# Prompt attention by pairs of heads, with the weights normalised by a diagonal in their transposes

## The chip, the core and the metric

The kernel runs on one core of a Trainium2 chip. The metric is the time of one execution on the device in microseconds. The core has TensorE (PE; its weight loads are PEld), VectorE (DVE), ScalarE (ACT), GpSimd (POOL) and SyncE (SP, which issues DMAs). They run side by side, each through its own instructions in order, and wait for each other on semaphores.

## The reference

One layer of a decoder for a prompt of 1024 tokens and 8 sampled sequences of 8 tokens, all f32, d_model 1024: an S5 state-space group and an attention with forget gates side by side, one output projection over both, then a mixture of 64 experts. What the change touches is the attention over the prompt (8 heads of 64) and the norm of its output:

```python
s = jnp.einsum('bqhd,bkhd->bhqk', q, k).astype(jnp.float32) * (HEAD_DIM ** -0.5)
s = s + jnp.transpose(cq, (0, 2, 1))[..., :, None] - jnp.transpose(ck, (0, 2, 1))[..., None, :]
causal = k_pos[None, :] <= q_pos[:, None]
s = jnp.where(causal, s, -jnp.inf)
p = jax.nn.softmax(s, axis=-1)
o = jnp.einsum('bhqk,bkhd->bqhd', p.astype(v.dtype), v)
...
merged = jnp.concatenate([_rmsnorm(y_ssm, g_ssm_out), _rmsnorm(o, g_attn_out)], axis=-1)
out = merged.astype(h.dtype) @ w_out
```

`cq` and `ck` are the running sums of the log forget values at queries and keys.

## The kernel before

The whole step is one program, its order on every engine written out by hand. The stages follow each other: state-space group, projections to q, k and v, attention over the prompt, attention of the sampled sequences over their pages, output projection, second norm, router, shared expert, routed experts.

PSUM is cut into six slots: 0 and 1 of two banks (1024 columns), 2 to 5 of one (512). `fill` makes TensorE wait until a slot's last content has been drained, `full` and `empty` count fillings and drainings, `wait_full` and `wait_empty` wait for a named one.

The attention over the prompt goes through 64 iterations `ATT`, for each head the eight query tiles i = 0 to 7, of (i + 1) x 128 keys. Four engines share one:
- TensorE (L714 to L748): `logits(it + 2)` into slot 0 or 1, with the whole 128 rows of `qT` (each head's copy of q has zeros in the other head's 64 rows) against `kT` of two heads; then, after a wait for the exponential, the transposes of the weights (L743, slots 2 and 3, four blocks each); then `weigh(it - 1)` (L728): transposed weights as stationary operand, v of 64 columns as moving one, into slot 4 or 5.
- VectorE (L1299 to L1320): logits plus running sum of the query minus that of the keys (L1313), the causal mask on the last 128 columns (L1316), the maximum (L1317), and the reciprocal of the previous iteration's sum (L1303).
- ScalarE (L1785 to L1812): the exponential with its sum (L1792, from `sc` into `pr`), the copies of the transposed weights (L1809), and the copy of the output of the iteration before, scaled by 1/sum (L1799), into `o_tok` (tokens by channels).
- `neg_c`, the keys' negated sums of one head spread over 128 partitions, is made once per head at i = 3: TensorE spreads it by an 8-row product into a logits slot (L707), ScalarE copies it (L1783).

GpSimd does nothing in this stage; before it, it clears `qT`, after it `q_bd` (L2016, the block-diagonal q of the samples), and later scales `w_out` by the norm's gains (L2021). The sampled sequences run through eight iterations (L784 to L813). Behind them, TensorE does the first half projection of tile 0 (`project_out(0, 0)`, the state-space half), while ScalarE squares `o_tok` (L1846), VectorE scales it by 1/rms (L1383), TensorE transposes it (L839) and ScalarE copies it into `oT` (L1853). Then come the other half projections (L830), two of 16 records per token tile. SyncE issues the shared expert's loads (L2184 to L2186) once the transposes are done. TensorE's first use of them is L864, in the third round of the second norm.

## Time and profile before

| | before |
|---|---|
| three runs | 2373.78, 2384.41 (median), 2386.98 us |
| the profiled execution | 2372.85 us, span 2371.1 us |
| PE busy | 2078.4 us (88%) |
| DVE, ACT, POOL busy | 892.5, 533.7, 300.3 us |

### The profile page before, as it was taken

Reading aid. Unit: us, or ns where it says so; the run is one execution under the profiler, and the core shown is the slowest. Engines: PE = TensorE matmul, PEld = TensorE weight load, DVE = VectorE, ACT = ScalarE, POOL = GpSimd, SP = SyncE. Lnnn points to the kernel's source line nnn. Section 1 sums busy time; section 2 is a strip of 40 time slices with the busy share of each in tenths; the row PEclk is TensorE's granted clock in tenths of the full one; section 3 lists DMA queues with packets and bytes.
Section 4 is the critical chain, followed back from the end, with each engine's and each line's share of the span. In section 5 each row is a group of like instructions: output and inputs, shape, how many; then the busy total and the mean of one; then the engine's idle time right before and its main releaser. Section 6 shows DMA issues by size and latency. Waiting matters only on the chain.

```text
span 2371.1 us, 28991 instructions
## 1 busy us (share of the span) xinstructions
PE 2078.4 (88%) x8262; PEld 1117.0 (47%) x8263; DVE 892.5 (38%) x2450; ACT 533.7 (23%) x993; POOL 300.3 (13%) x236
## 2 busy tenths in 40 slices
PE   4797899998888888978978999899899999998990
PEld 1456555446666334545434444444445455544450
DVE  2827400315554222234423333333333333333338
ACT  3423221015544112033111111111111111111122
POOL 0010100000000030000001122122122222221124
PEclk7898889999998998988988999999899999999995
DMA  9531200022000443001148899899888778898843
GB/s 335 218 155 23 113 0 1 0 76 58 18 1 18 131 138 133 0 19 58 52 176 279 288 298 293 277 295 297 265 273 250 250 241 259 266 288 281 287 102 137
DMA packets 100878, 394.20 MB, mean 166 GB/s; under 512 B 27279, under 2 KB 30003, under 8 KB 71996
## 3 DMA queue, kind: packets, MB, share of 16 engines
q1 hardware_dynamic: 70020, 302.44, 34.4%
q0 software_dynamic: 24768, 90.19, 15.9%
q10 hardware_dynamic: 6024, 0.73, 0.2%
q8 instruction: 38, 0.62, 0.1%
q14 instruction: 28, 0.23, 0.0%
HBM read 329.16 MB, written 62.57 MB: 165 GB/s over the span
## 4 chain that ended last, share of the span: by engine, by line
PE 27%; DMA 22%; issue 5%; SPq 4%; DVE 2%; ACT 1%; POOL 0%; POOLq 0%; DVEq 0%; ACTq 0%
DMA arena<-in_w_exp_down 22%; PE psum L961 11%; PE psum L989 5%; PE psum L830 5%; SPq L2209 2%; PE psum L947 1%; SPq L2204 1%; SPq L2205 1%; DVE arena L1607 1%; PE psum L858 1%; PE psum L864 1%; DVE arena L1617 1%; PE psum L871 0%; PE psum L809 0%; PE psum L854 0%
## 5 line engine op out<-in xcount | busy, mean ns | idle before, releaser
L961 PE MATMUL psum<-arena 128*128 x1360 | 631.1, 619 | 55.2 <-SPq L2230 51.5
L961 PEld LDWEIGHTS psum<-arena 128*128 128x128 f32 x1360 | 261.1, 197 | 358.3 <-issue 358.3
L989 PE MATMUL psum<-arena,tail 128*128 x672 | 302.3, 592 | 0.0
L2057 POOL DMA_INDIRECT moe_rows<-arena x84 | 133.4, 1588 | 815.2 <-ACT arena L1941 291.4
L1563 DVE TENSOR_TENSOR arena<-arena,psum 128x256 f32<-128x256 f32 x85 | 35.8, 421 | 499.2 <-ACT arena L1927 499.2
L989 PEld LDWEIGHTS psum<-arena,tail 128*128 128x128 f32 x672 | 121.1, 190 | 120.5 <-issue 120.5
L1927 ACT ACTIVATE arena<-psum 128x256 f32<-128x256 f32 x85 | 32.7, 385 | 644.3 <-PE psum L961 644.3
L678 PE MATMUL psum<-arena 128*128 128x512 f32 (+1 forms) x384 | 126.5, 493 | 0.0
L830 PE MATMUL psum<-arena 128*128 128x512 f32 (+1 forms) x288 | 124.3, 593 | 0.9 <-ACT arena L1853 0.5
L1541 DVE TENSOR_TENSOR arena<-tail,arena 128x1152 bf16<-128x1152 f32 x89 | 119.6, 1344 | 0.0
L1941 ACT ACTIVATE arena<-psum,arena 128x512 f32<-128x512 f32 x84 | 57.7, 687 | 213.3 <-PE psum L989 213.3
L947 PEld LDWEIGHTS psum<-tail,arena 128*128 128x128 f32 x688 | 81.1, 142 | 52.2 <-issue 44.8
L1590 DVE TENSOR_SCALAR arena<-psum,arena 128x512 f32<-128x512 f32 x84 | 63.1, 751 | 95.9 <-PE psum L989 95.9
L1922 ACT ACTIVATE arena<-psum 128x1024 f32<-128x1024 f32 x86 | 88.1, 1024 | 48.9 <-PE psum L947 48.9
L719 PE MATMUL psum<-arena 128*128 128x512 f32 (+2 forms) x192 | 86.9, 569 | 10.4 <-ACT arena L1783 10.4
L947 PE MATMUL psum<-tail,arena 128*128 128x128 f32 x688 | 90.1, 274 | 6.5 <-DMA arena<-h_rows,arena 6.5
L830 PEld LDWEIGHTS psum<-arena 128*128 128x128 f32 (+1 forms) x288 | 68.5, 239 | 55.3 <-issue 40.1
L2044 POOL DMA_INDIRECT arena<-h_rows,arena x88 | 86.6, 984 | 59.4 <-issue 32.2
L678 PEld LDWEIGHTS psum<-arena 128*128 128x128 f32 x384 | 63.8, 193 | 62.6 <-issue 62.6
L728 PE MATMUL psum<-arena 128*128 128x64 f32 x576 | 77.2, 284 | 0.0
L728 PEld LDWEIGHTS psum<-arena 128*128 128x128 f32 x576 | 75.3, 206 | 0.0
L544 PE MATMUL psum<-arena 128*128 128x512 f32 (+1 forms) x144 | 65.0, 604 | 0.0
(486 smaller groups left out, 2342.1 us busy)
## 6 DMA issues: line engine op xcount, KB each, us to landing
arena<-in_w_exp_gate SPq DMA_DIRECT2D x64, 1024.0 KB, 5.3
arena<-in_w_exp_up SPq DMA_DIRECT2D x64, 1024.0 KB, 9.4
arena<-in_w_exp_down SPq DMA_DIRECT2D x64, 1024.0 KB, 12.3
arena<-in_w_ada SPq DMA_DIRECT2D x24, 1024.0 KB, 7.6
arena<-in_w_ada_final SPq DMA_DIRECT2D x8, 1024.0 KB, 6.5
arena<-in_cache_k SPq DMA_DIRECT2D x32, 256.0 KB, 3.4
arena<-in_cache_v SPq DMA_DIRECT2D x32, 256.0 KB, 2.9
arena<-in_w_in SPq DMA_DIRECT2D x1, 6176.0 KB, 18.5
```

The source lines that it names most:

```text
L544: ins = pe.matmul(slot[2 + t % 2][0:rows(t), :], tile_of(hT, t, k), w_u[:, k, :], start=(k == 0), stop=(k == KD - 1))
L678: ins = pe.matmul(slot[b][:, 0:c1 - c0], w_q[:, k, w * DA + j * P:w * DA + (j + 1) * P], hT[:, k, c0:c1], start=(k == 0), stop=(k == KD - 1))
L719: ins = pe.matmul(slot[it % 2][:, c0:c1], qT[:, h, i * P:(i + 1) * P], kT[:, h // 2, c0:c1], start=True, stop=True)
L728: ins = pe.matmul(slot[4 + it % 2][:, 0:DH], pt[:, it % 2, j * P:(j + 1) * P], v[:, j, h * DH:(h + 1) * DH], start=(j == 0), stop=(j == i))
L830: ins = pe.matmul(slot[half][0:rows(t), n * 512:(n + 1) * 512], lhs, w_out[:, half * KA + k, n * 512:(n + 1) * 512], start=(k == 0), stop= ...
L947: ins = pe.transpose(slot[0][:, k * P:(k + 1) * P], x_rows[:, par, k * P:(k + 1) * P], ident)
L961: ins = pe.matmul(slot[2 + par].rearrange("p (h n) -> p h n", h=2), xTs[:, par, k, :], ring_gu[:, at, :, k, :].rearrange("p a h n -> p (a ...
L989: ins = pe.matmul(slot[1][:, n * 512:(n + 1) * 512], hTs[:, k, :], ring_d[:, at, k, n, :].rearrange("p a n -> p (a n)"), start=(k == 0), s ...
L1541: tt(onehot[:, par], iota_row.unsqueeze(1).to_broadcast([P, NT, P]), blk_rank[:, par].unsqueeze(2).to_broadcast([P, NT, P]), ALU.is_equal) ...
L1922: f(xTs[:, par].rearrange("p k c -> p (k c)"), slot[0], ACT.Copy).then_inc(xt_copied, 1)
L2044: pool.indirect_dma_start(x_rows[:, par, :], None, h2_dram, bass.IndirectOffsetOnAxis(ap=g_idx[:, par:par + 1], axis=0)).then_inc(gathered ...
L2057: pool.indirect_dma_start(y_dram, bass.IndirectOffsetOnAxis(ap=s_idx[:, par:par + 1], axis=0), y_buf[:, par, :], None, compute_op=ALU.add) ...
```

## The change

The attention goes by pairs of heads j (two heads share the 128 rows of `qT` and `kT`) and, within a pair of heads, by tiles of falling width, i = 7 to 0: 32 pairs p, 64 numbers it = 2 p + a.
- Logits: one product of 64 rows for each head, in alternation, head a in slot a. `qT` has no zeros any more (the clearing by GpSimd and half of ScalarE's q copies go).
- The mask: GpSimd adds it to the 128 diagonal columns of `neg_c` before each tile (falling widths make this sound), of which there are now four buffers; VectorE's add of it goes.
- The exponential works in place in `sc` (four buffers). VectorE makes the reciprocal of the sum behind its add for the next pair, GpSimd multiplies the identity by it (`over_sum`), and TensorE's products of the weights with this diagonal transpose and normalise them.
- Weighing: v is the stationary operand (64 columns) and the transposed weights the moving one; the two heads write the two halves of the 128 PSUM partitions, so the output is in `oT` (channels by tokens) with one copy per pair.
- The spreading of the sums is cut in halves of 512 columns, in slots 4 and 5: four ahead of the loop, the others behind the pairs with i = 6, 5, 4, 3.
- The norm: `o_tok`, its squares, its scaling and its transposes go, but for the 64 sampled rows (`o_smp`). GpSimd squares `oT` and adds over the channels' four blocks under the sampled sequences, TensorE sums over partitions with eight products of one column in iteration b = 4, and VectorE multiplies the attention half of the projection by 1/rms where it adds it.
- SyncE issues the shared expert's loads behind the last projection instead of ahead of the second.

The core of the diff; runs of removed lines are left out, the functions above show them.

```diff
-        qT = arena(21536, H, T)
+        qT = arena(21536, KA, T)
         v = arena(30240, NT, DA)
         kT = arena(41248, KA, T)
         k_tok = arena(45600, 2, DA)
         lf = arena(46624, T, parts=H)
         lf_a = arena(47712, T, parts=H)
...
+        sc = arena(8192, 4, SEQ)
+        pt = arena(25888, 4, SEQ)
+        oT = arena(14336, KA, T)
+        o_smp = arena(18944, DA, parts=NS)
+        o_acc = arena(39200, SEQ)
+        o_pow = arena(40512, 512)
+        over_sum = arena(40512, 4, P)
         c_row = arena(18944, T, parts=H)
-        neg_c = [arena(20032, SEQ), arena(39200, SEQ)]
+        neg_c = [arena(20032, SEQ), arena(39200, SEQ), arena(12288, SEQ), arena(13312, SEQ)]
...
-        ATT = [(i, h) for h in range(H) for i in range(8)]
+        PAIRS = [(i, j) for j in range(KA) for i in range(7, -1, -1)]
...
+        SPREAD_AT = (6, 5, 4, 3)
+        def pt_keys(p):
+            return range(0, PAIRS[p][0] + 1, 4)
+        def spread_of(p):
+            i, j = PAIRS[p]
+            if j + 1 == KA or i not in SPREAD_AT:
+                return None
+            a, n = divmod(SPREAD_AT.index(i), 2)
+            return 2 * (j + 1) + a, n
...
+            def spread_sums(h, n, s_):
+                fill(pe, ("CB", h, n), s_)
+                full(pe.matmul(slot[s_], ident[0:H, h:h + 1].to_broadcast([H, P]), c_row[:, n * 512:(n + 1) * 512], start=True, stop=True), ("CB", h, n))
+            for i in range(4):
+                spread_sums(i // 2, i % 2, 4 + i % 2)
             slots.wait_empty(pe, ("V", 7))
...
+            def logits(p):
+                i, j = PAIRS[p]
+                for a in range(2):
+                    fill(pe, ("L", 2 * p + a), a)
                 for c0 in range(0, (i + 1) * P, 512):
                     c1 = min(c0 + 512, (i + 1) * P)
...
+                    for a in range(2):
+                        h0, h1 = a * DH, (a + 1) * DH
+                        ins = pe.matmul(slot[a][:, c0:c1], qT[h0:h1, j, i * P:(i + 1) * P], kT[h0:h1, j, c0:c1], start=True, stop=True)
+                        if c1 == (i + 1) * P:
+                            full(ins, ("L", 2 * p + a))
+            def turn_weights(p, a):
+                i, j = PAIRS[p]
+                it = 2 * p + a
+                pe.wait_ge(pn_ready, it + 1)
+                for q0 in pt_keys(p):
                     b = 2 + (q0 // 4)
                     fill(pe, ("PT", it, q0), b)
-                    for j in range(q0, min(q0 + 4, i + 1)):
-                        ins = pe.transpose(slot[b][:, (j - q0) * P:(j - q0 + 1) * P], pr[:, it % 2, j * P:(j + 1) * P], ident)
+                    for m in range(q0, min(q0 + 4, i + 1)):
+                        ins = pe.matmul(slot[b][:, (m - q0) * P:(m - q0 + 1) * P], sc[:, it % 4, m * P:(m + 1) * P], over_sum[:, it % 4, :], start=True, stop=True)
                     full(ins, ("PT", it, q0))
...
+            def weigh(p):
+                i, j = PAIRS[p]
+                fill(pe, ("O", p), 4 + p % 2)
+                for m in range(i + 1):
+                    for a in range(2):
+                        if m % 4 == 0:
+                            slots.wait_empty(pe, ("PT", 2 * p + a, m))
+                        ins = pe.matmul(slot[4 + p % 2][a * DH:(a + 1) * DH, 0:P], v[:, m, (2 * j + a) * DH:(2 * j + a + 1) * DH],
+                                        pt[:, (2 * p + a) % 4, m * P:(m + 1) * P], start=(m == 0), stop=(m == i), skip_group_check=True)
+                full(ins, ("O", p))
+            logits(0)
+            for p in range(len(PAIRS)):
+                if p + 1 < len(PAIRS):
+                    logits(p + 1)
+                turn_weights(p, 0)
+                if p:
+                    weigh(p - 1)
+                turn_weights(p, 1)
+                if spread_of(p):
+                    spread_sums(*spread_of(p), 4 + (p + 1) % 2)
+            weigh(len(PAIRS) - 1)
...
+                if b == 4:
+                    pe.wait_ge(o_squares, 1)
+                    fill(pe, "OSS", 4)
+                    for t in range(8):
+                        ins = pe.matmul(slot[4][:, t:t + 1], o_acc.rearrange("p (c t) -> p t c", t=CH)[:, t], ones_col, start=True, stop=True)
+                    full(ins, "OSS")
...
+            slots.wait_empty(pe, "SR")
+            fill(pe, "OT", 2)
+            for k in range(KA):
+                ins = pe.transpose(slot[2][:, k * P:k * P + NS], o_smp[:, k * P:(k + 1) * P], ident[0:NS, 0:NS])
+            full(ins, "OT")
             for t in range(NT):
                 if t:
                     project_out(t, 0)
+                if t == 8:
+                    slots.wait_empty(pe, "OT")
...
             def one_over_sum(it):
                 dve.wait_ge(p_ready, it + 1)
                 if it >= 4:
...
+                    dve.wait_ge(pn_ready, it - 3)
+                dve.reciprocal(att_one[:, 8 + it % 4:9 + it % 4], att_one[:, 4 + it % 4:5 + it % 4]).then_inc(recip_ready, 1)
+            for p, (i, j) in enumerate(PAIRS):
                 n = (i + 1) * P
...
+                for a in range(2):
+                    it = 2 * p + a
+                    full(dve, ("L", it))
+                    dve.wait_ge(c_masked, it + 1)
+                    if it >= 4:
+                        full(dve, ("PT", it - 4, pt_keys(p - 2)[-1]))
+                    empty(stt(sc[:, it % 4, 0:n], slot[a][:, 0:n], c_tok[:, i * H + 2 * j + a:i * H + 2 * j + a + 1], neg_c[(2 * j + a) % 4][:, 0:n], ALU.add, ALU.add), ("L", it))
+                    if p:
+                        one_over_sum(it - 2)
+                for a in range(2):
+                    it = 2 * p + a
+                    slots.wait_empty(dve, ("L", it))
+                    dve.tensor_reduce(att_one[:, it % 4:it % 4 + 1], sc[:, it % 4, 0:n], AX.X, ALU.max, negate=True).then_inc(s_ready, 1)
+            for it in (2 * len(PAIRS) - 2, 2 * len(PAIRS) - 1):
+                one_over_sum(it)
...
+            dve.wait_ge(o_sq, 1)
             dlink(ts(ssq, ssq, 1.0 / DA, EPS, ALU.mult, ALU.add))
             dve.sem_inc(x_var, 1)
             dve.wait_ge(x_std, NXG + 1)
             dlink(dve.reciprocal(rstd, rstd))
...
-                ins = tt(mix, mix, slot[1][0:m, :], ALU.add)
+                ins = stt(mix, slot[1][0:m, :], rstd[0:m, t:t + 1], mix, ALU.mult, ALU.add)
...
+            def spread_out(h, n):
+                full(act, ("CB", h, n))
+                if h >= 4:
+                    act.wait_ge(s_ready, 16 * (h // 2 - 1))
+                empty(f(neg_c[h % 4][:, n * 512:(n + 1) * 512], slot[slots.use[("CB", h, n)][0]], ACT.Copy, scale=-1.0), ("CB", h, n))
             def exponentials(it):
-                n = (ATT[it][0] + 1) * P
+                n = (PAIRS[it // 2][0] + 1) * P
                 act.wait_ge(s_ready, it + 1)
-                if it >= 2:
-                    full(act, ("PT", it - 2, pt_keys(it - 2)[-1]))
                 if it >= 4:
                     act.wait_ge(recip_ready, it - 3)
...
+                f(sc[:, it % 4, 0:n], sc[:, it % 4, 0:n], ACT.Exp, bias=att_one[:, it % 4:it % 4 + 1],
+                  accum_out=att_one[:, 4 + it % 4:5 + it % 4]).then_inc(p_ready, 1)
+            def weights_out(it):
+                p = it // 2
+                for q0 in pt_keys(p):
+                    w = min(4, PAIRS[p][0] + 1 - q0) * P
                     full(act, ("PT", it, q0))
...
+                    if p >= 2:
+                        full(act, ("O", p - 2))
+                    empty(f(pt[:, it % 4, q0 * P:q0 * P + w], slot[2 + q0 // 4][:, 0:w], ACT.Copy), ("PT", it, q0))
+            def attention_out(p):
+                i, j = PAIRS[p]
+                full(act, ("O", p))
+                empty(f(oT[:, j, i * P:(i + 1) * P], slot[4 + p % 2][:, 0:P], ACT.Copy), ("O", p))
+            for i in range(4):
+                spread_out(i // 2, i % 2)
+            for p in range(len(PAIRS) + 1):
+                for a in range(2):
+                    if p < len(PAIRS):
+                        exponentials(2 * p + a)
+                    if p:
+                        weights_out(2 * p - 2 + a)
+                if p >= 2:
+                    attention_out(p - 2)
+                if p and spread_of(p - 1):
+                    spread_out(*spread_of(p - 1))
+            attention_out(len(PAIRS) - 1)
...
+            slots.wait_empty(act, "SR")
+            slots.wait_empty(act, "OSS")
+            f(sq_o[0:NS, :], o_smp, ACT.Square, accum_out=ssq[0:NS, 8:9]).then_inc(o_sq, 1)
...
+            def mask(p):
+                i, j = PAIRS[p]
+                for a in range(2):
+                    h = 2 * j + a
+                    if i == 7:
+                        slots.wait_empty(pool, ("CB", h, 0))
+                        slots.wait_empty(pool, ("CB", h, 1))
+                    else:
+                        slots.wait_empty(pool, ("L", 2 * p - 2 + a))
+                    diag = neg_c[h % 4][:, i * P:(i + 1) * P]
+                    pool.tensor_tensor(diag, diag, causal, ALU.add).then_inc(c_masked, 1)
+            def spread_diagonal(it):
+                pool.wait_ge(recip_ready, it + 1)
+                if it >= 4:
+                    slots.wait_full(pool, ("PT", it - 4, pt_keys(it // 2 - 2)[-1]))
+                pool.tensor_scalar(over_sum[:, it % 4, :], ident, att_one[:, 8 + it % 4:9 + it % 4], None, ALU.mult).then_inc(pn_ready, 1)
+            for p in range(len(PAIRS) + 1):
+                if p < len(PAIRS):
+                    mask(p)
+                if p:
+                    spread_diagonal(2 * p - 2)
+                    spread_diagonal(2 * p - 1)
+            slots.wait_full(pool, ("O", len(PAIRS) - 1))
             plink(pool.memset(q_bd[:, :, :, :], 0.0))
             pool.sem_inc(smp_pool, 1)
+            slots.wait_empty(pool, ("O", len(PAIRS) - 1))
+            slots.wait_empty(pool, ("O", len(PAIRS) - 2))
+            for n in range(2):
+                cols = slice(512 * n, 512 * (n + 1))
+                plink(pool.tensor_tensor(o_acc[:, cols], oT[:, 0, cols], oT[:, 0, cols], ALU.mult))
+                for j in range(1, KA):
+                    plink(pool.tensor_tensor(o_pow, oT[:, j, cols], oT[:, j, cols], ALU.mult))
+                    plink(pool.tensor_tensor(o_acc[:, cols], o_acc[:, cols], o_pow, ALU.add))
+            pool.sem_inc(o_squares, 1)
...
-            slots.wait_full(sp, ("OT", 8))
-            slots.wait_full(sp, ("OT", 7))
+            slots.wait_full(sp, ("W", NT - 1, 1))
             dma(sh_gu[:, :, 0:FE], ap["w_sh_gate"][0].rearrange("(k p) n -> p k n", p=P)).then_inc(ld_shared, 16)
             dma(sh_gu[:, :, FE:], ap["w_sh_up"][0].rearrange("(k p) n -> p k n", p=P)).then_inc(ld_shared, 16)
             dma(sh_d, ap["w_sh_down"][0].rearrange("(k p) n -> p k n", p=P)).then_inc(ld_shared, 16)
-            slots.wait_full(sp, ("W", NT - 1, 1))
```

## Rows read from the trace of the kernel before

**Rows 1.** Stages of TensorE's middle part, by windows.

```profile
core 0: us, PE busy (x) PEld busy (x) DVE busy (x) ACT busy (x) POOL busy (x), PEclk, DMA share, GB/s
529.20:759.30 230.10, 201.80 (x1085) 144.25 (x1086) 124.56 (x256) 117.86 (x295) 0.36 (x1) 0.90 0.07 20
909.80:923.10 13.30, 6.48 (x37) 4.86 (x37) 4.03 (x11) 7.05 (x14) 0.00 (x0) 0.74 0.07 22
```

**Rows 2.** Groups by shape, 529.2 to 759.4 us: busy us, mean ns, idle before.

```profile
L1809 ACT ACTIVATE arena<-psum 128x512 f32<-128x512 f32 x48 | 27.9, 597 | 63.5 <-PE psum L743 63.5
L1809 ACT ACTIVATE arena<-psum 128x128 f32<-128x128 f32 x16 | 4.4, 274 | 3.7 <-PE psum L743 3.7
L1316 DVE TENSOR_TENSOR arena<-arena,tail 128x128 f32<-128x128 f32 x64 | 18.7, 292 | 2.2
L1792 ACT ACTIVATION_READ_ACCUMULATOR arena<-arena,tail 128x1 f32 x64 | 12.2, 191 | 0.0
L1303 DVE RECIPROCAL tail<-tail 128x1 f32<-128x1 f32 x64 | 10.3, 161 | 73.5 <-ACT arena L1792 73.4
L1313 DVE SCALAR_TENSOR_TENSOR arena<-psum,arena 128x1024 f32<-128x1024 f32 x8 | 10.3, 1284 | 2.9 <-PE psum L719 2.9
L1313 DVE SCALAR_TENSOR_TENSOR arena<-psum,arena 128x128 f32<-128x128 f32 x8 | 2.8, 350 | 4.2 <-PE psum L719 4.2
L1317 DVE TENSOR_REDUCE tail<-arena 128x1 f32<-128x1024 f32 x8 | 9.8, 1220 | 0.3
L1317 DVE TENSOR_REDUCE tail<-arena 128x1 f32<-128x128 f32 x8 | 2.3, 286 | 0.3
L1792 ACT ACTIVATE arena<-arena,tail 128x1024 f32<-128x1024 f32 x8 | 9.1, 1138 | 0.1
L1792 ACT ACTIVATE arena<-arena,tail 128x128 f32<-128x128 f32 x8 | 3.1, 391 | 0.7 <-DVE tail L1317 0.7
```

**Rows 3.** Timeline (start, us), weight loads of transposes and weighing, widest tile.

```profile
727.40 0.85 PEld L743 LDWEIGHTS psum<-tail,arena 128*128 128x128 f32 x8 [1.44 <-ACT arena L1792]
730.86 1.86 PEld L728 LDWEIGHTS psum<-arena 128*128 128x128 f32 x16
```

**Rows 4.** Timeline, spreading of the sums, first and last of seven.

```profile
537.37 1.98 PE L707 MATMUL psum<-arena,tail 8*128 8x512 f32 x4
...
709.34 1.98 PE L707 MATMUL psum<-arena,tail 8*128 8x512 f32 x4
```

**Rows 5.** A window inside L602, and the timeline of half-height products.

```profile
204.00:206.00 2.00, 2.00 (x39) 2.00 (x37) 1.02 (x3) 1.74 (x5) 0.00 (x0) 1.00 0.07 8
...
243.22 2.06 PE L622 MATMUL psum<-arena 64*128 64x128 f32 x32
```

**Rows 6.** Timeline, products of 128, of 8 and again of 128 rows.

```profile
779.88 3.65 PE L809 MATMUL psum<-arena 128*64 128x512 f32 x8 [0.72 <-ACT arena L1836]
783.46 1.07 PE L810 MATMUL psum<-arena 8*64 8x512 f32 x2
784.46 3.65 PE L787 MATMUL psum<-arena 128*64 128x512 f32 x8
```

**Rows 7.** Groups by shape on GpSimd, whole span.

```profile
L2067 POOL TENSOR_TENSOR arena<-arena 128x1024 f32<-128x1024 f32 x8 | 24.2, 3022 | 34.9 <-DVE arena L1617 34.9
L2021 POOL TENSOR_SCALAR arena<-arena,tail 128x1024 f32<-128x1024 f32 x8 | 22.8, 2845 | 101.1 <-DMA arena<-in_w_out 100.5
L1995 POOL TENSOR_SCALAR tail<-tail 128x72 f32<-128x72 f32 x3 | 1.2, 406 | 0.3
```

**Rows 8.** Windows of 2 us in the third head, around its spreading.

```profile
596.00:598.00 2.00, 0.68 (x6) 0.55 (x6) 0.00 (x0) 1.98 (x4) 0.00 (x0) 0.99 0.52 134
598.00:600.00 2.00, 2.00 (x3) 0.97 (x4) 0.16 (x1) 0.63 (x2) 0.00 (x0) 0.50 0.00 0
```

**Rows 9.** DMA issues from 915 to 1070 us, with KB and us to landing.

```profile
arena<-in_w_sh_down SPq DMA_DIRECT2D x1, 1024.0 KB, 10.9
```

**Rows 10.** Timeline, first product that reads the shared expert's weights.

```profile
1066.36 2.02 PE L864 MATMUL psum<-arena 128*128 128x512 f32 x2
```

141 lines of the change are left out of this document (17 added, 124 removed).

## The prediction

> **What bounds the kernel now.** I read the stages first, by windows of the trace. The attention over the prompt runs from 529.2 to 759.3, 230.1 us, with TensorE's mean granted clock at 0.90 [rows 1]; the change rewrites this stage. Behind it come the sampled sequences and then a stretch of 13.3 us (909.8 to 923.1) in which the attention's rows are squared, scaled and transposed and TensorE has 6.5 us of work [rows 1]. Then comes the output projection. In front and behind TensorE has no wait that the change touches. All of this lies one after another, so what the stage and the stretch gain or lose is gained or lost in the span, until the experts, which only start earlier or later.
>
> Inside the stage no engine is full: VectorE is busy 124.6 us, ScalarE 117.9 [rows 1]. The second view is the groups by shape [rows 2]. Let b be the width of a query tile's keys in blocks of 128 (1 to 8). Per head and tile: the add of logits on VectorE takes 0.22 + 0.133 b us (0.350 at 1 block, 1.284 at 8), the maximum 0.16 + 0.133 b, the exponential with the read of its sum about 0.38 + 0.107 b, the copy of transposed weights 0.17 + 0.108 b up to b = 4 (0.60), the reciprocal 0.16 [rows 2]. One head returns after (709.34 - 537.37) / 6 = 28.66 us [rows 4], two heads after 57.3; that is what a column of eight pairs must beat.
>
> **TensorE's prices.** An f32 product is two records; one of 512 columns takes 0.43 us at full clock (8 in 3.65, less its tail) [rows 6], so 0.107 us for 128 columns. A transpose is one record: 8 loads in 0.85 us, 0.107 each; a product bound by its 128 by 128 weights costs 0.115 per record (16 in 1.86) [rows 3]. Two half arrays overlap: products of 136 columns with 64 output columns, in alternating halves, come at 39 in 2 us, 0.051 each, where one alone would take 0.113; and 32 products of half height alternate at 2.06 / 32 = 0.064 [rows 5].
>
> **The change on TensorE, per column of two heads** (36 blocks). Transposes by a diagonal become products: 2 heads x 36 x 0.23 = 16.6 us instead of 7.7. Weighing is 4 x 36 records of 128 columns at half width, 0.0535 each: 7.7 instead of 16.6. Logits in halves: 0.213 us per block and pair, 7.7 instead of 15.4. Spreading the sums is 3.4 as before. The sum falls from 43.1 to 35.4, 31 us in four columns. That is work, and the path is work and waits.
>
> **New cost 1, changes between forms.** Behind 8 products of 128 rows the first of 8 rows starts 3.58 us later (3.42 of work), and the way back costs 1.00 for 0.85 [rows 6]: 0.15 each; I take 0.13, since the products here are short. Bounds 0 and 0.16. Three per pair are exposed: 0.39 x 32 = 12.5 us. A rule of the Trainium skill speaks against the change here: TensorEngine Tiling (Array Packing), Key Properties, says that a change of the tiling mode drains the engine. By that rule the trace agrees, with 0.15.
>
> **New cost 2, GpSimd in the chain.** No row has its 128 by 128 operations. By 2845 ns for 1024 columns a scaling would be 0.36, by 406 ns for 72 columns up to 0.55 [rows 7]; I take 0.45 (bounds 0.3 and 0.6, 5 us over 32 pairs either way). The adding of the mask, at 3022 / 8 = 0.38 [rows 7], waits for nothing late: GpSimd does it an iteration ahead. It takes 0.292 of VectorE per tile and head away [rows 2], 18.7 us in all.
>
> **The chain of an iteration.** TensorE's order for pair p is: logits of p+1, transposes of its first head, weighing of p-1, transposes of the second. VectorE takes the reciprocal of pair p only behind its add for p+1, which needs those logits. So TensorE stands between the logits and the first transposes. Let t be the start of VectorE's add for pair p+1, of n blocks. First transposes: t + (0.22 + 0.133 n) + 0.19 (reciprocal) + 0.07 + 0.45 (diagonal) + 0.07 = t + 1.0 + 0.133 n. They take 0.23 b; a form change and the weighing follow (0.214 per block of p-1), and another change. The second head's transposes also need the first's copied out, and ScalarE has the exponential of p+1 queued ahead of that copy: two adds, two reciprocals, a maximum, the exponential and the copy end at t + 2.10 + 0.506 n (1.78 for b = 1). Then 0.23 b, a change, and the next logits (0.213 per block, 0.17 until seen) give the next t.
>
> Tiles come with b = 8, 7, ..., 1, and the eight periods are 9.1, 8.4, 7.3, 6.3, 5.3, 4.3, 4.9 and 7.8 us: 53.4 for a column. For example b = 5 (n = 4, before it 6, after next 3): first transposes at 1.53, ended 2.68, weighing 2.81 to 4.09, second from 4.22 (ScalarE ready at 4.12) to 5.37, logits 0.13 + 0.64 + 0.17 later: 6.31. At b = 1 the exponential is of the next column's 8 blocks, and the second transposes wait until 5.8.
>
> Spreading the sums adds to that. It is now four pieces in b = 7, 6, 5, 4 of three columns, and each takes the PSUM bank that the weighing of p-1 has just left, whose copy ScalarE makes behind all copies of the pair. TensorE waits 1.0 us, works 0.86, and gets its clear run 1.8 us late: 12 x 1.8 = 21.6.
>
> **The stage.** Eight pieces of spreading instead of four put the first logits at 531; two adds and two maxima of eight blocks have to pass before the first reciprocal, so the first t of a full iteration is 538.8. Four columns are 213.6, spreading 21.6, and the last two iterations' 12.8 shrink to 5.2, as nothing follows: end at 766.4, 7.1 us later than now, at full clock throughout.
>
> **The clock.** It is at 0.99 in one window and 0.50 in the next, behind a stretch in which TensorE had only eight-row products and few others [rows 8]. At 0.90 the stage spends 20% of its time, 46 us, at the 1.2 GHz level [rows 1], about 5.7 us behind each of seven spreadings and the end. In the changed kernel I see 16 such places: 12 spreadings (wait 1.0, spread 0.86, about 1 us of logits, wait 1.7 before the transposes) and four column ends. A place costs 5.7 x 0.5 x 0.6 (the path's share of TensorE work), 1.7 us. My 7.1 has none of them, so 0 to 27 us are to be added. Their stretches are as long as the present one (4.6 us) but hold more full-height work; I take two in three, 18 us.
>
> **Behind the stage.** The squares go to GpSimd under the sampled sequences (14 products of 512 columns at half of 3.02 us [rows 7], 21 us; only the scaling of w_out stands behind them in its queue, and that waits for its loads until 862 anyway). TensorE sums them in iteration 4: 16 records at 0.115 and a wait for a drain, 2.2 us, part of it beside a wait for ScalarE: +1.5. The 13.3 us stretch shrinks to four transposes of the sampled rows, 0.6: -12.7. What hid it is gone with it; next late would be the first projections' copy, which ScalarE can do 5 us ahead. The 1/rms moves into VectorE's add per tile, 1.3 us beside 13 us of projection: nothing. Eight chained copies for the samples lose their chain: -0.5. The clearing of qT and the halved q copies (24 become 12) lie beside projections that never wait: nothing. The shared expert's three loads are issued behind the last projection instead of before the first; the last lands 10.9 us after its issue [rows 9], so by 1053, and is wanted at 1066 [rows 10]: nothing, or up to 5 us if the DMA engines are shared.
>
> **Sum.** +7.1 + 18 + 1.5 - 12.7 - 0.5 = +13.4. The profiled execution took 2372.85 us (span 2371.1), 11.6 below the median of the three runs, 2384.41. On the profile's basis that is 2386, on the median's 2398, and I predict 2398. Its own range, from the bounds of GpSimd, the spreading's wait (0.4 x 12) and the clock, is 2384 to 2413.
>
> **Rivals.** (1) The clock holds in the new stage, since the stretches carry full products. For it: 128-row products replace transposes. Against it: [rows 8]. The sum is then -4.6: 2380, no difference, and this is the case that is not slower; it decides from fewer than 3 falls. (2) As (1), and the changes of form are hidden, too, because between 128-column products there is time to load: -12.5 more, 2367, faster. Against it: both rows of 0.15 [rows 6]. (3) Half arrays do not overlap in this order, in which only two records of one half alternate with two of the other: logits and weighing then cost up to twice, 15.4 x 4 = 61 us more. Half of that gives 2428. Against it: [rows 5], measured on such alternation.
>
> **How the numbers follow.** Chances: forecast 0.52, (1) 0.23, (2) 0.13, (3) 0.12. Reaching down to (2) and up to (3), 2366 to 2430 leaves 2 in 10 out. A change of under 0.5% (12 us) can't be told from none here. Of the forecast's own range 0.36 lies above 2396.3 and 0.16 below; of (1), 0.06 falls under 2372.5. Faster: 0.06 + 0.13 = 0.19; same: 0.16 + 0.17 = 0.33; slower: 0.36 + 0.12 = 0.48.
>
> **What would show it.** A column of pairs of 60 us or more with spreading and 53 without; TensorE idle 1.8 to 2.2 us before the first transposes of a wide pair, released by GpSimd; 1 us before each spreading, released by ScalarE; diagonals of 0.45 us; a granted clock of 0.83 to 0.88 in the stage; projections back to back from the sampled sequences on. I am wrong if GpSimd's operations take 1 us, if the idle time before the transposes is missing, or if the clock stays above 0.93.

## The result and the profile after

The changed kernel takes 2416.93 us (median of four runs, 2410.35 to 2419.56); the kernel before took 2379.59 beside it (2373.78 to 2386.98). The ratio is 1.0151, with a 95% interval of 1.0109 to 1.0193. So it is slower by 1.5%, 26 to 46 us. The forecast of +13.4 us had the side right and the size far too small.

The profiled execution took 2414.41 us (span 2412.6). Its page, part 1 (busy us and share by engine):

```profile
PE 2087.2 (87%) x8534; PEld 1126.6 (47%) x8535; DVE 866.1 (36%) x2378; ACT 509.9 (21%) x933; POOL 374.4 (16%) x377
```

VectorE and ScalarE have less to do than before (892.5 and 533.7), GpSimd more (300.3), TensorE 9 us more. Its stages by windows, in order: spreading and attention up to the last weighing, the transition, the sampled sequences, the projection, norm and router, and the experts (us; engines' busy time with the number of records; TensorE's granted clock; DMA share; GB/s).

```profile
528.30:811.90 283.60, 212.19 (x1376) 152.02 (x1376) 95.75 (x192) 110.98 (x272) 68.35 (x134) 0.82 0.06 16
811.90:825.00 13.10, 2.66 (x23) 2.18 (x21) 11.27 (x18) 1.30 (x2) 11.95 (x10) 0.74 0.26 80
825.00:969.90 144.90, 127.37 (x456) 53.15 (x457) 32.38 (x73) 18.84 (x40) 28.91 (x14) 0.87 0.38 122
969.90:1095.50 125.60, 125.60 (x294) 69.20 (x292) 30.24 (x26) 18.48 (x24) 0.00 (x0) 0.99 0.06 25
1095.50:1281.30 185.80, 148.20 (x619) 87.14 (x618) 78.15 (x317) 49.09 (x77) 9.92 (x13) 0.88 0.24 91
1281.30:2412.60 1131.30, 1026.18 (x3695) 513.79 (x3695) 430.40 (x1406) 195.93 (x288) 243.26 (x178) 0.95 0.81 262
```

The kernel before cut in the same way, first two rows and last row:

```profile
525.30:759.30 234.00, 204.51 (x1092) 144.91 (x1091) 125.02 (x258) 119.00 (x296) 3.63 (x6) 0.90 0.08 20
759.30:767.40 8.10, 3.48 (x20) 3.16 (x18) 6.14 (x18) 1.34 (x2) 1.81 (x1) 0.71 0.29 76
...
1226.80:2371.10 1144.30, 1029.39 (x3695) 514.23 (x3695) 430.82 (x1407) 195.98 (x288) 243.23 (x178) 0.95 0.80 259
```

A second profile of the kernel before (the run before_again below) tells how far one execution can be trusted. All in us:

| part | before | before, again | after |
|---|---|---|---|
| up to the first spreading | 525.3 | 527.8 | 528.3 |
| spreading and attention | 234.0 | 244.2 | 283.6 |
| transition | 8.1 | 7.9 | 13.1 |
| sampled sequences | 135.5 | 135.4 | 144.9 |
| norm stretch and projection | 137.4 | 137.7 | 125.6 |
| second norm to shared expert | 186.5 | 185.8 | 185.8 |
| routed experts | 1144.3 | 1136.5 | 1131.3 |

Against the mean of the two, the attention loses 44.5 us, the sampled sequences 9.5, the transition 5.1 and the start 1.8. The norm and projection gain 12.0. The experts' 9.1 are no gain of the change: in the variants of the changed kernel below this part takes 1122 to 1144 us.

In the attention TensorE is busy for 212 us instead of 205, at a lower clock. The groups, by shape, that answer to [rows 2]:

```profile
L744 PE MATMUL psum<-arena 128*128 128x128 f32 x576 | 100.3, 331 | 59.4 <-POOL arena L2049 51.4 <-ACT arena L1821 8.0
L2049 POOL TENSOR_SCALAR arena<-tail 128x128 f32<-128x128 f32 x64 | 38.3, 603 | 204.2 <-DVE tail L1329 203.7
L2043 POOL TENSOR_TENSOR arena<-arena,tail 128x128 f32<-128x128 f32 x64 | 27.9, 455 | 8.3 <-DVE arena L1339 4.3 <-ACT arena L1804 3.9
L717 PE MATMUL psum<-arena,tail 8*128 8x512 f32 x32 | 20.6, 748 | 9.8 <-ACT arena L1826 9.3 <-DVE arena L1322 0.6
L1339 DVE SCALAR_TENSOR_TENSOR arena<-psum,arena 128x1024 f32<-128x1024 f32 x8 | 10.1, 1277 | 23.2 <-PE psum L732 23.2
L1345 DVE TENSOR_REDUCE tail<-arena 128x1 f32<-128x1024 f32 x8 | 9.3, 1207 | 0.0
```

TensorE stands still for 59.4 us ahead of the transposing products (L744): 51.4 until GpSimd's diagonal (L2049), in 31 of the 32 pairs, and 8.0 until ScalarE's copy. In the kernel before, the transposes had to wait, too, but only for 19.1 us:

```profile
L743 PE MATMUL psum<-tail,arena 128*128 128x128 f32 x288 | 48.0, 298 | 19.1 <-ACT arena L1792 18.5
```

All of TensorE's idle time in the stage grew from 29.5 us (234.0 - 204.5) to 71.4 (283.6 - 212.2). The timeline of a pair's end and a column's end shows all of the chain:

```profile
600.09 0.35 DVE L1339 SCALAR_TENSOR_TENSOR arena<-psum,arena 128x128 f32<-128x128 f32 x1 [4.40 <-PE psum L732]
600.36 0.15 DVE L1329 RECIPROCAL tail<-tail 128x1 f32<-128x1 f32 x1
600.61 1.18 POOL L2049 TENSOR_SCALAR arena<-tail 128x128 f32<-128x128 f32 x2 [4.00 <-DVE tail L1329]
601.26 0.71 PE L744 MATMUL psum<-arena 128*128 128x128 f32 x4 [1.21 <-POOL arena L2049]
601.91 0.88 PE L754 MATMUL psum<-arena 128*64 128x128 f32 x12
602.71 0.71 PE L744 MATMUL psum<-arena 128*128 128x128 f32 x4
603.35 1.99 PE L732 MATMUL psum<-arena 64*128 64x512 f32 x8
605.37 1.28 DVE L1339 SCALAR_TENSOR_TENSOR arena<-psum,arena 128x1024 f32<-128x1024 f32 x1 [4.17 <-PE psum L732]
606.57 0.15 DVE L1329 RECIPROCAL tail<-tail 128x1 f32<-128x1 f32 x1
606.83 0.60 POOL L2049 TENSOR_SCALAR arena<-tail 128x128 f32<-128x128 f32 x1 [4.20 <-DVE tail L1329]
607.48 0.49 PE L744 MATMUL psum<-arena 128*128 128x128 f32 x2 [2.14 <-POOL arena L2049]
...
609.13 1.15 ACT L1811 ACTIVATE arena<-arena,tail 128x1024 f32<-128x1024 f32 x1 [5.12 <-DVE tail L1345]
610.28 0.26 ACT L1821 ACTIVATE arena<-psum 128x128 f32<-128x128 f32 x1
610.68 0.77 PE L744 MATMUL psum<-arena 128*128 128x128 f32 x2 [2.12 <-ACT arena L1821]
```

After the logits (603.35 to 605.34) come an add of 1.28 us, the reciprocal, 0.60 us of GpSimd, and TensorE has stood for 2.14 us. At the column's end the copy of one block waits behind the exponential of eight (609.13), and TensorE stands for 2.12 us once more. The three changes of form can be read here, too: four records of 0.115 take 0.64 us up to the next form (602.71 to 603.35), twelve of 0.053 take 0.80 (601.91 to 602.71). That is 0.16 to 0.18 each. And the half arrays overlap: eight records of 512 columns take 1.99 us.

### The profile page after: what moved, and what is told of

Same layout as the page of the kernel before. It is cut to its first block, busy times and chain, and to the rows that moved or that the text cites. A ratio compares the mean times of both kernels' runs of the same rounds, so it can differ in the third digit from the quotient of the medians.

```text
span 2412.6 us, 29543 instructions
## 1 busy us (share of the span) xinstructions
PE 2087.2 (87%) x8534; PEld 1126.6 (47%) x8535; DVE 866.1 (36%) x2378; ACT 509.9 (21%) x933; POOL 374.4 (16%) x377
## 4 chain that ended last, share of the span: by engine, by line
PE 27%; DMA 22%; issue 5%; SPq 4%; DVE 2%; ACT 1%; POOL 0%; POOLq 0%; DVEq 0%; ACTq 0%
DMA arena<-in_w_exp_down 21%; PE psum L987 11%; PE psum L1015 5%; PE psum L857 5%; SPq L2260 2%; PE psum L973 1%; SPq L2255 1%; SPq L2256 1%; DVE arena L1631 1%; PE psum L884 1%; PE psum L836 1%; PE psum L890 1%; PE psum L897 1%; DVE arena L1641 1%; PE psum L880 0%
## 5 line engine op out<-in xcount | busy, mean ns | idle before, releaser
L987 PEld LDWEIGHTS psum<-arena 128*128 128x128 f32 x1360 | 260.1, 196 | 347.0 <-issue 347.0
L744 PE MATMUL psum<-arena 128*128 128x128 f32 x576 | 100.3, 331 | 59.4 <-POOL arena L2049 51.4
L689 PE MATMUL psum<-arena 128*128 128x512 f32 (+1 forms) x384 | 126.7, 493 | 0.0
L744 PEld LDWEIGHTS psum<-arena 128*128 128x128 f32 x576 | 86.4, 232 | 84.0 <-POOL arena L2049 69.7
L857 PE MATMUL psum<-arena 128*128 128x512 f32 (+1 forms) x288 | 125.2, 597 | 0.0
L1339 DVE SCALAR_TENSOR_TENSOR arena<-psum,arena 128x1024 f32<-128x1024 f32 (+7 forms) x64 | 51.3, 809 | 183.4 <-PE psum L732 183.4
L1942 ACT ACTIVATE arena<-psum 128x1024 f32<-128x1024 f32 x86 | 88.1, 1024 | 46.7 <-PE psum L973 46.7
L689 PEld LDWEIGHTS psum<-arena 128*128 128x128 f32 x384 | 63.9, 193 | 62.6 <-issue 62.6
L2049 POOL TENSOR_SCALAR arena<-tail 128x128 f32<-128x128 f32 x64 | 38.3, 603 | 204.2 <-DVE tail L1329 203.7
```

Source lines behind the costliest of these rows:

```text
L689: ins = pe.matmul(slot[b][:, 0:c1 - c0], w_q[:, k, w * DA + j * P:w * DA + (j + 1) * P], hT[:, k, c0:c1], start=(k == 0), stop=(k == KD - 1))
L744: ins = pe.matmul(slot[b][:, (m - q0) * P:(m - q0 + 1) * P], sc[:, it % 4, m * P:(m + 1) * P], over_sum[:, it % 4, :], start=True, stop=True)
L857: ins = pe.matmul(slot[half][0:rows(t), n * 512:(n + 1) * 512], lhs, w_out[:, half * KA + k, n * 512:(n + 1) * 512], start=(k == 0), stop= ...
L987: ins = pe.matmul(slot[2 + par].rearrange("p (h n) -> p h n", h=2), xTs[:, par, k, :], ring_gu[:, at, :, k, :].rearrange("p a h n -> p (a ...
L1942: f(xTs[:, par].rearrange("p k c -> p (k c)"), slot[0], ACT.Copy).then_inc(xt_copied, 1)
```

## The experiments

Every kernel below is the changed one with the edit shown. Ratios are to the kernel before, run on the same chip beside it; the changed kernel's own is 1.0151. Only ratios can be compared between the runs: the kernel before had medians of 2365.8 to 2372.4 us beside them, and 2379.6 beside the changed kernel. Where a stage is given, it is cut as in the table above.

**Reciprocals ahead of the add** (recip_first).

```diff
                 for a in range(2):
                     it = 2 * p + a
+                    if p:
+                        one_over_sum(it - 2)
                     full(dve, ("L", it))
...
-                    if p:
-                        one_over_sum(it - 2)
```

> VectorE takes the reciprocal of pair p's sum ahead of its add for pair p+1 instead of behind it; nothing else is changed. Theory (TensorE stands between the logits of p+1 and the first transposes of p because the reciprocal is queued behind an add of up to 1.28 us that needs those logits; such waits also lower the granted clock): the reciprocal and GpSimd's diagonal then run beside the logits, TensorE's 59 us of idle time before the transposing products fall below 25, the attention over the prompt gets 25 to 45 us shorter and its granted clock rises from 0.81 to 0.87 or more; total 2375 to 2390, back to about the kernel before. Rival A (the exponential is the late one anyway, the reciprocal only rides along): under 8 us. Rival B (the clock falls whatever TensorE waits for in this order): 15 to 25 us shorter with the clock still at 0.80 to 0.83.

Ratio 0.9981 (0.9949 to 1.0014), 2365.01 us. The attention took 240.2 us instead of 283.6, and the clock was 0.89. Its window and the group of the transposing products:

```profile
527.80:768.00 240.20, 191.52 (x1376) 133.79 (x1376) 98.92 (x192) 108.23 (x272) 69.05 (x134) 0.89 0.07 19
...
L744 PE MATMUL psum<-arena 128*128 128x128 f32 x576 | 87.5, 301 | 36.6 <-ACT arena L1821 35.5 <-POOL arena L2049 0.6
```

The theory holds: the wait for GpSimd falls from 51.4 to 0.6 us. The idle time was expected to fall below 25 us; it fell to 36.6. Some 27 us more of it now end with ScalarE's copy, which frees the bank for the next transposes and stands behind an exponential. Of the 43 us gained, 23 are idle time; the other 21 are TensorE's records getting shorter at a higher clock (its busy time falls from 212 to 192 us for the same 1376 records). In the total the gain is 1.7%, some 40 us.

**Spreading into a bank that has long been drained** (spread_bank).

```diff
-                    spread_sums(*spread_of(p), 4 + (p + 1) % 2)
+                    spread_sums(*spread_of(p), 4 + p % 2)
```

> Each piece of spreading is written to the bank that the weighing of pair p-2 used, which has been copied out long ago, instead of the bank of p-1. Theory: the 12 waits of about 1.0 us ahead of the spreading go, and their falls of the clock grow rarer: 12 us by the waits alone, 10 to 18 with the clock; total 2399 to 2407. Rival (the time moves into the next wait, ahead of the first transposes, since ScalarE and VectorE are no earlier): under 4 us.

Ratio 1.0060 (1.0022 to 1.0097), 2383.1 us: 0.9% under the changed kernel, some 21 us. The attention took 256.9 us, 26.7 less, at a clock of 0.88. The groups:

```profile
L717 PE MATMUL psum<-arena,tail 8*128 8x512 f32 x32 | 20.6, 748 | 0.6 <-DVE arena L1322 0.6
...
L744 PE MATMUL psum<-arena 128*128 128x128 f32 x576 | 91.0, 309 | 60.7 <-POOL arena L2049 51.4 <-ACT arena L1821 9.3
```

The waits ahead of the spreading are gone (9.8 to 0.6), and the wait ahead of the transposes hasn't taken their place (60.7 against 59.4). Waits of 9 us in all were worth 27 us of the stage, more than was expected (10 to 18).

**Squares later** (squares_late). GpSimd waits for `smp_q` before it squares.

```diff
             slots.wait_empty(pool, ("O", len(PAIRS) - 2))
+            pool.wait_ge(smp_q, 1)
             for n in range(2):
```

> GpSimd starts the squares of the attention's rows only once VectorE has made the sampled queries' block diagonal, some 13 us later. Theory (GpSimd's two-input operations in SBUF slow VectorE's in the transition: 602 ns for a copy of 64 by 64 that takes 225 in the kernel before): the stretch from the last weighing to the first product of the sampled sequences goes from 12.9 us back to 8 or 9, VectorE's copies of queries take 0.2 to 0.25 us each, total 4 us less (2413). Rival (VectorE's copies are slow because they now lie on half of the partitions or behind the clearing of the block diagonal): transition unchanged. In the sampled sequences' first iterations the small VectorE operations may be slowed instead: up to 3 us given back.

The transition took 8.0 us instead of 13.1, and nothing was given back in the sampled sequences (142.8 us against 144.9). VectorE's eight copies of q and a small scaling ahead of them, without and with GpSimd's squares beside them (this run, then the changed kernel; groups by line):

```profile
L1365 DVE COPY arena<-arena 64x64 f32<-64x64 f32 x8 | 1.5, 189 | 0.2
L1360 DVE TENSOR_SCALAR tail<-tail 64x8 f32<-64x8 f32 x1 | 0.2, 223 | 0.0
...
L1365 DVE COPY arena<-arena 64x64 f32<-64x64 f32 x8 | 4.8, 602 | 0.2
L1360 DVE TENSOR_SCALAR tail<-tail 64x8 f32<-64x8 f32 x1 | 1.1, 1119 | 0.0
```

So the 5 us come from GpSimd working in SBUF at the same time, not from the half partitions. The ratio is 1.0168 (1.0111 to 1.0225), no different from 1.0151: 5 us are less than such a comparison can tell.

**Work added: products in the wait** (filler). In all pairs but the first, ahead of the wait for the diagonal.

```diff
+                if a == 0 and p:
+                    fill(pe, ("O", p - 1), 4 + (p - 1) % 2)
+                    for _ in range(5):
+                        pe.matmul(slot[4 + (p - 1) % 2][:, 256:384], ident, ident, start=True, stop=True)
                 pe.wait_ge(pn_ready, it + 1)
...
-                fill(pe, ("O", p), 4 + p % 2)
+                if p + 1 == len(PAIRS):
+                    fill(pe, ("O", p), 4 + p % 2)
```

> Work is added: 31 times, ahead of the wait for the first transposes of a pair, TensorE makes five extra products of 128 by 128 (1.15 us at full clock) that nobody reads, in columns of a bank that is free. Theory of the clock (the waits in the stage lower the granted clock, and that is what the forecast mis-sized): the extra products fit into the wait of about 1.9 us, the granted clock of the stage rises from 0.81 to 0.88 or more, and the stage gets 8 to 25 us shorter although it does more: 2392 to 2409. Rival (the clock doesn't go by these waits): clock as before, stage the same or up to 15 us longer where the clock is low: 2416 to 2432.

Ratio 1.0073 (1.0039 to 1.0108), 2386.71 us. With 310 more records the attention is 26.9 us shorter:

```profile
529.70:786.40 256.70, 223.93 (x1686) 164.92 (x1686) 95.71 (x192) 109.42 (x272) 68.29 (x134) 0.94 0.07 18
...
L748 PE MATMUL psum<-arena 128*128 128x128 f32 x576 | 82.3, 289 | 20.8 <-POOL arena L2054 11.1 <-ACT arena L1826 9.6
L742 PE MATMUL psum<-tail 128*128 128x128 f32 x310 | 45.3, 296 | 0.0
```

Nothing on VectorE, ScalarE or GpSimd was changed. What changed is that TensorE had products in the place of waits, and its granted clock rose from 0.82 to 0.94. In the total the gain is 0.8%, some 18 us. This is the strongest evidence that the waits cost through the clock, beside their own length.

**The kernel before, once more** (before_again). No edit.

> The kernel before, profiled once more, to see how much a stage differs between two executions of one kernel. Two readings of the 13.6 us by which everything behind the output projection was shorter after the change. If the loads of the experts' weights just fell better in that execution, a second profile of the kernel before gives some 1317 us for this part and the two kernels don't differ there; if the change does it (by a later start of the experts, say), it gives 1328 to 1333 us again, as the four variants of the changed kernel agree within 5 us there. The attention stage should repeat within 2 us.

2377.14 us, span 2375.3. Everything behind the output projection took 1322.3 us, between the two readings (some 1317 in the changed kernel, 1330.8 in the first profile). The experts alone took 1136.5 us against 1144.3, and over all variants they spread from 1122 to 1144, so their difference can't be put down to the change. The attention didn't repeat within 2 us as expected: 244.2 against 234.0 us. Its middle, cut to the same 230.1 us as [rows 1], has a clock of 0.88 against 0.90.

```profile
531.80:761.90 230.10, 202.48 (x1046) 143.36 (x1046) 124.82 (x255) 115.97 (x290) 0.28 (x1) 0.88 0.07 20
```

A stage whose clock falls and rises has no fixed length: 10 us lie between two executions. The changes of 27 and 43 us above are well beyond that; one of 5 us in such a stage isn't.

**Sums of squares in four parts** (sums_split). The 16 records of the sums, in one piece in sequence 4, go to sequences 4 to 7, ahead of the wait for ScalarE's copy.

```diff
+                if b >= 4:
+                    if b == 4:
+                        pe.wait_ge(o_squares, 1)
+                    fill(pe, ("OSS", b), 4)
+                    for t in (2 * b - 8, 2 * b - 7):
+                        ins = pe.matmul(slot[4][:, t:t + 1], o_acc.rearrange("p (c t) -> p t c", t=CH)[:, t], ones_col, start=True, stop=True)
+                    full(ins, ("OSS", b))
                 slots.wait_empty(pe, ("SP", b))
...
+                if b >= 4:
+                    full(dve, ("OSS", b))
+                    empty(cp(ssq[:, 2 * b - 8:2 * b - 6], slot[4][:, 2 * b - 8:2 * b - 6]), ("OSS", b))
```

> The sums of squares (16 products of one column, 1.84 us at full clock) are no longer taken in one piece behind the logits of sampled sequence 4, but two tiles each in sequences 4 to 7, ahead of TensorE's wait for ScalarE's copy of the turned weights, which is 1.0 us long already. Theory (in one piece they are followed by TensorE at the 1.2 GHz level up to the end of that sequence: 23.4 us against 15.2 to 16.9 for the others): sequence 4 takes 17 us or less, the sampled sequences 137 to 139 us instead of 144, total 5 to 7 us less. Rival (any product of so few columns in this loop brings the clock down, four places cost as much as one): 144 us again or more.

This run speaks for the rival. The sampled sequences took 143.0 us instead of 144.9, and the ratio is 1.0179 (1.0132 to 1.0226); the last run below limits what follows from it. Sequence 4 falls from 23.6 to 17.1 us, but 5 and 6 now take 17.1 each instead of 15.2, and the sequences 1 to 3 ahead of them 16.8 each, as they did. In the changed kernel TensorE is at 0.72 while it takes the sums and works through the rest of sequence 4 (windows of the 42 us in front of sequence 4, and of that sequence):

```profile
855.00:897.00 42.00, 38.49 (x135) 13.91 (x133) 8.74 (x19) 4.66 (x10) 0.00 (x0) 0.91 0.51 159
897.00:921.00 24.00, 22.41 (x80) 12.03 (x79) 4.26 (x10) 2.44 (x5) 0.00 (x0) 0.72 0.40 140
```

**The diagonal on VectorE** (diag_vectore). GpSimd's part of it goes.

```diff
                 dve.reciprocal(att_one[:, 8 + it % 4:9 + it % 4], att_one[:, 4 + it % 4:5 + it % 4]).then_inc(recip_ready, 1)
+                dve.wait_ge(recip_ready, it + 1)
+                ts(over_sum[:, it % 4, :], ident, att_one[:, 8 + it % 4:9 + it % 4], None, ALU.mult).then_inc(pn_ready, 1)
```

> VectorE makes the diagonal of reciprocals itself, right behind its reciprocal; GpSimd only adds the masks. Theory (GpSimd's 0.60 us and the two hand-overs lie in full between the reciprocal and the first transposes, in all 32 pairs): VectorE needs about 0.2 us for it, the wait shortens by 0.4 to 0.5 us a pair, 13 to 16 us of TensorE's 59 us of idle time, and with the clock 14 to 25 us of the total. Rival (VectorE's queue is what is late: two more instructions per pair ahead of the maxima delay the exponentials by what they save): under 6 us.

The rival holds: ratio 1.0180 (1.0137 to 1.0223), no gain; the attention took 294.9 us. VectorE's diagonal isn't 0.2 us. It takes 0.51 us where GpSimd adds masks at the same time and 0.29 where it doesn't. The timeline of VectorE and the masks:

```profile
594.27 0.45 POOL L2045 TENSOR_TENSOR arena<-arena,tail 128x128 f32<-128x128 f32 x1 [8.54 <-DVE arena L1341]
594.30 0.51 DVE L1331 TENSOR_SCALAR arena<-tail 128x128 f32<-128x128 f32 x1
...
601.22 0.29 DVE L1331 TENSOR_SCALAR arena<-tail 128x128 f32<-128x128 f32 x1
```

And the two extra instructions of a pair stand ahead of its maxima, so the wait moved to ScalarE's copies: TensorE's idle time is 45.7 us until VectorE (in the changed kernel 51.4 until GpSimd) and 20.3 until ScalarE (8.0). Taking the diagonal off GpSimd brought nothing, while moving the reciprocal brought 43 us of the stage. Since VectorE's diagonal is hardly shorter than GpSimd's 0.60, this run doesn't say what a really short one would bring.

**Four edits together** (combined): recip_first, spread_bank, squares_late, sums_split.

> Four edits together: reciprocals ahead of the add, spreading into the long drained bank, squares behind the queries' block diagonal, sums of squares in four parts. Theory (they remove different waits; the spreading's and the reciprocal's lie behind one another): attention under 232 us at a granted clock of 0.91 or more, transition 8 us, sampled sequences 138 us; against the kernel before a ratio of 0.982 to 0.990, so some 2330 to 2350. Rival (the first two edits remove the same time, since ScalarE's copies are next in both): attention 238 to 242 us as with the reciprocals alone, ratio 0.992 to 0.995.

Ratio 0.9901 (0.9859 to 0.9943), 2347.83 us: faster than both kernels, at the weak end of what was expected. The attention took 230.0 us at 0.90, the transition 7.9, the sampled sequences 143.6. The sampled sequences were not at the expected 138. The spreading's edit still gave 10 us beside the reciprocals' (240.2 to 230.0), which is no more than the two profiles of before differ.

**Two banks for narrow pairs, sums in the projection** (banks). On top of combined, without the four parts:

```diff
-                    b = 2 + (q0 // 4)
+                    b = 2 + (q0 // 4 if i >= 4 else a)
...
-                    empty(f(pt[:, it % 4, q0 * P:q0 * P + w], slot[2 + q0 // 4][:, 0:w], ACT.Copy), ("PT", it, q0))
+                    empty(f(pt[:, it % 4, q0 * P:q0 * P + w], slot[slots.use[("PT", it, q0)][0]][:, 0:w], ACT.Copy), ("PT", it, q0))
```

and the sums' eight products stand behind `project_out(0, 0)` (with `o_acc` and `o_pow` in another place).

> The combined kernel with two changes. (a) The sums of squares are taken in one piece again, but behind the first of the output's projections instead of within the sampled sequences, whose loop then holds what it held before the change. Theory (products of one column cost this loop its clock, in one piece or in four): the sampled sequences take 135 to 137 us instead of 143.6, the projection at most 2 us more; total 5 to 8 us less. Rival (the loop is longer for another reason, such as the squares on GpSimd or w_out's scaling beside it): 143 us again. (b) In pairs of four blocks or fewer the two heads' turned weights go to different banks instead of one. Theory (TensorE's 36 us of idle time before the first transposes are the wait for ScalarE to copy out the bank of the pair before, behind an exponential): the narrow half of each column no longer waits, 5 to 10 us less in the attention, 220 to 226 us. Rival (the wait is then for the copies that the weighing reads): under 3 us. Against the kernel before a ratio of 0.982 to 0.987.

Ratio 0.9866 (0.9812 to 0.9919). The banks: the attention took 210.0 us at 0.94 instead of 230.0 at 0.90, and the idle time of the transposing products fell from 37.2 to 27.1 us. That is twice the upper end of what was expected, again with the clock. The sums: the sampled sequences took 138.7 us without them, nearer to the theory's 135 to 137 than to the rival's 143, but the projection took 130.1 instead of 124.4 in combined, 3.7 of it the sums themselves at the lower clock, and what follows 192.0 instead of 184.5. So moving them gained nothing here.

**And another order on ScalarE** (banks_order): as banks, both heads' copies ahead of the second exponential.

```diff
-                for a in range(2):
-                    if p < len(PAIRS):
-                        exponentials(2 * p + a)
-                    if p:
-                        weights_out(2 * p - 2 + a)
+                if p < len(PAIRS):
+                    exponentials(2 * p)
+                if p:
+                    weights_out(2 * p - 2)
+                    weights_out(2 * p - 1)
+                if p < len(PAIRS):
+                    exponentials(2 * p + 1)
```

> As the run with two banks, and ScalarE also copies out the turned weights of both heads of the pair before ahead of the second head's exponential, instead of one before and one behind it. Theory (the copy that frees the bank stands behind an exponential of up to 1.14 us, READ of the sum included 1.3): TensorE's wait before the first transposes of the wide pairs falls by some 1 us each, 10 to 16 us less in the attention than with the banks alone. Rival (the second exponential then comes later by these copies, and with it its reciprocal, diagonal and the second head's transposes, so that the wait changes its place): within 4 us of the run with banks alone, or longer at the column ends.

Ratio 0.9856 (0.9814 to 0.9897), attention 211.5 us, idle 28.3: the rival holds, nothing is gained. Behind the sampled sequences this run takes 321.5 us up to the experts, as banks does (322.1).

**The best of these** (best): combined with the two banks.

> The combined kernel (sums of squares in four parts within the sampled sequences, which moved to the projection cost as much there) with the two banks for the turned weights of narrow pairs. If the stages add up as measured in the other runs, the attention takes 210 us as in the run with the banks, the transition 8, the sampled sequences 143.6 and the rest 305 to 309 up to the experts, so 20 us less than the combined kernel: 2322 to 2332, a ratio of 0.980 to 0.985 to the kernel before. If the 13 us by which the part behind the sampled sequences was longer in the run with the banks comes from the attention's earlier end instead of the moved sums, the projection and what follows take 320 us again and the ratio is 0.986 to 0.988.

Ratio 0.9839 (0.9805 to 0.9874), 2330.43 us. Attention, transition, sampled sequences and the part up to the experts:

```profile
526.80:734.40 207.60, 179.04 (x1376) 126.73 (x1376) 99.20 (x192) 107.99 (x272) 69.02 (x134) 0.94 0.09 22
734.40:742.30 7.90, 2.64 (x23) 2.18 (x21) 6.10 (x18) 1.30 (x2) 3.22 (x3) 1.00 0.36 102
742.30:880.10 137.80, 121.99 (x456) 49.99 (x457) 32.66 (x76) 18.87 (x41) 37.27 (x21) 0.91 0.38 126
880.10:1185.70 305.60, 267.50 (x909) 150.99 (x909) 108.46 (x343) 67.32 (x100) 9.95 (x13) 0.95 0.18 68
```

The stages add up, the first of the two readings: behind the sampled sequences it is 305.6 us again, so the 16 us more in the two runs before go with the sums behind the projection. The attention by pairs takes 207.6 us here, against 234.0 and 244.2 in the kernel before: the idea was good, and its waits ate it.

The same sums in four parts lie in a loop of 137.8 us here and of 143.0 and 143.6 in the two others, at 0.91 against 0.87. The sequences 4 to 6, with sums, take 17.1 us each in all three. What differs most are the sequences 1 to 3, without sums: 15.2 each here, 16.8 in the two others, and the kernel before has sequences of both lengths, too. So most of these 5 us have a reason other than the sums, which no run settles. The price of the sums in four parts stays open, by these lengths between 0.3 and 1.9 us for each sequence, an estimate.

## Why the forecast was right in side and wrong in size

- **TensorE's work.** Right. Half arrays overlap (1.99 us for eight records of 512 columns), records of the weighing come at 0.053 us (20 weight loads in 1.07). Rival (3) is excluded.
- **The chain of an iteration.** Right, in its order and nearly in its sizes. The idle time ahead of the first transposes was forecast at 1.8 to 2.2 us for a wide pair. It is 1.97 us at b = 8 and 2.14 in the row of 607.48, beside an add of eight blocks. Where the clock was high the periods fit: at b = 8 the add starts at 544.78 and 553.45, 8.67 us for a forecast of 9.1; at b = 4, with spreading, at 586.37 and 593.94, 7.57 us for 7.1. At the column's end both waits came as forecast, but the period was 9.4 us for 7.8.
- **GpSimd's diagonal.** Mis-sized: 0.603 us, at the upper bound and not at 0.45. 32 x 0.15 is 5 us. The mask took 0.455 us for 0.38 and waited for nothing late, as forecast. The lower price was drawn from a long operation; by the two measured scalings (0.603 us at 128 columns, 2.845 at 1024) some 0.28 us of each doesn't shrink with the columns, an estimate.
- **Changes of form.** Each took 0.16 to 0.18 us, forecast were 0.13: 96 x 0.04, 4 us. Rival (2), which had them hidden, is wrong in this, too. The rule of the Trainium skill that was cited (TensorEngine Tiling (Array Packing), Key Properties) speaks of a drain at each change of mode; the trace agrees, with these sizes.
- **Spreading.** The wait was forecast at 1.0 us; it is 9.3 us ahead of L717 for twelve, 0.8 each (1.0 by the weight loads, 11.6 for twelve). The first four pieces had been priced at the full clock (first logits 1.8 us later than in the kernel before, at 531). They took 7.19 us at the 1.2 GHz level, and the first logits came at 535.5. Of these 4.5 us, 1.5 are the clock; 3.0 are only the later start of the stage in this execution (528.3 against 525.3), and by the profiles the start lies anywhere between 520.4 and 529.7.

```profile
528.33 7.19 PE L717 MATMUL psum<-arena,tail 8*128 8x512 f32 x8 [0.58 <-DVE arena L1322]
```

- **The clock. This is the step that failed.** The forecast gave it 18 us, two thirds of an upper end of 27, which was 1.7 us for each of 16 places. The stage without it was to end at 766.4 and ended at 811.9. 4.5 us of that are the later first logits, 5 the diagonal, 4 the forms; some 32 are left for the clock, by subtraction. Worked back from the mean clock ((1 - 0.82) / 0.5 = 36% of 283.6 us), 102 us lay at the 1.2 GHz level. At the forecast's own price (x 0.5 x 0.6) they are 31 us, so the price of a microsecond at that level fits, and what was wrong is how many there are: the kernel before has 47 and 68 us in its two profiles, the forecast's 18 us stand for two thirds of 91 (16 places of 5.7), which is its upper end. Two things were wrong. The argument for a discount (the stretches are as long as before but fuller) was a guess against [rows 8], and the granted clock came out at 0.82, under the 0.83 to 0.88 that were to show the forecast right. And only spreadings and column ends were counted as places, while every pair has a wait of 1.2 to 2.1 us. Taking away the twelve waits of the spreading gave 27 us of the stage, filling 31 of the others with useless products gave 27 as well, and both brought the clock up (0.88, 0.94); in the total it was 21 and 18 us.

```profile
544.78:614.77 69.99, 50.32 (x341) 35.99 (x340) 23.96 (x48) 27.40 (x69) 16.28 (x32) 0.87 0.23 63
614.77:689.08 74.31, 55.71 (x344) 41.14 (x344) 23.86 (x48) 27.43 (x68) 16.23 (x32) 0.78 0.00 1
689.08:761.91 72.83, 54.23 (x344) 39.15 (x344) 23.86 (x48) 27.59 (x68) 16.25 (x32) 0.80 0.00 1
```

  These are three columns of the changed kernel, each with four spreadings: 70.0, 74.3 and 72.8 us, for 53.4 + 4 x 1.8 = 60.6 at the full clock. The longest has the lowest clock.
- **Rivals (1) and (2).** Wrong: the clock didn't hold. The filler run shows what they had in mind: with TensorE kept busy, the stage wins back 27 of the 44.5 us that it had lost.
- **Behind the stage.** The norm: -12.7 forecast, -12.0 found. The sums in the loop: +1.5 forecast, and the loop is 9.5 longer. The sequence with them is 23.6 us instead of 15.2 or 16.8; their 1.84 us of work and what follows in it have a mean clock of 0.72. Again the work was priced and the clock left out. How much of the 9.5 the sums are stays open: without them the loop took 138.7 us in banks, some 3 more than in the kernel before.
- **The q copies: wrong in sign.** A gain of 0.5 us from losing their chain was forecast; the transition became 5.1 us longer, since the squares on GpSimd run beside VectorE's short operations. The forecast put 14 operations on GpSimd "under the sampled sequences" and asked only what waits for them, not what they slow. The Trainium skill has the rule that would have warned (GPSIMD Engine Reference, section 8, Key points): GpSimd shares its SBUF interfaces with VectorE, and they contend where VectorE's instruction is in a 2-port mode or has two inputs in SBUF. The trace agrees with the contention (602 against 189 ns); in which of the two cases the copies are, no run here shows.
- **Shared expert's loads.** Nothing, as forecast: 185.8 us against 186.5 and 185.8.

The change was forecast at +13.4 us and is +37.3 by the medians. The forecast's own range (2384 to 2413) ends below the measured 2416.93, and it was drawn too narrow: the bounds that it names (5 us for GpSimd, 4.8 for the spreading's wait, 0 to 27 for the clock) add up to some 2370 to 2417. That the measured time lies inside the wider range, up to 2430, is luck: that end was set by rival (3), which the traces exclude. The chance of 0.48 for slower had 0.12 from it.

The sum was +13.4; against the mean of two profiles of before the stages up to the experts add up to +48.5, and the experts' -9.1, which isn't the change's, brings the span to +39.4.

## What to carry over

Before an engine is put between a reduction and TensorE, write down what the instruction that feeds it stands behind in its queue: here a reciprocal moved over one add was worth 43 us of the stage (40 of the total), and a bank with an older content 27 (21). In this loop a wait of TensorE cost its own length and then the clock behind it (9 us of waits were worth 27), so every wait of the loop is priced with the granted clock in view, not only the conspicuous ones. Where a stage has a changing clock, read two profiles of the kernel before you trust its length: the same stage took 234.0 and 244.2 us.

## What the runs showed of the hardware

- Useless products in the place of waits made the stage 26.9 us shorter; granted clock 0.82 to 0.94.
- A scaling of 128 by 128 on GpSimd takes 0.603 us, an add of that size 0.455, a product of 128 by 512 1.04 to 1.29.
- Beside GpSimd's two-input operations in SBUF, some of VectorE's operations within SBUF take up to five times as long: 64 by 64 copies 602 ns for 189, a scaling of 64 by 520 1.08 us for 0.42, one of 64 by 8 1.12 us for 0.22, the diagonal 0.51 for 0.29. Others beside them don't change: the sums of 64 by 8 (0.15 us in both) and the copies out of PSUM (two of 128 by 512 in 1.29 us in both).
- TensorE changes between whole and half arrays at 0.16 to 0.18 us each, with products of 128 columns.
